# Second scores and new values that wait for fewer VectorE operations, and squares' sums in two pieces

## The reference, cut to what matters

```python
def l2norm(x):
    return x * lax.rsqrt(jnp.sum(x * x, axis=-1, keepdims=True) + EPS)

def gated_delta_rule(q, k, v, g, beta):        # q, k: l2norm of silu(conv(h @ w))
    G = jnp.cumsum(gc, axis=-1)
    decay = jnp.exp(jnp.where(incl, G[..., :, None] - G[..., None, :], -jnp.inf))
    kk = jnp.einsum("bhnid,bhnjd->bhnij", kc, kc)
    a_mat = jnp.where(strict, bc[..., :, None] * kk * decay, 0.0) + jnp.eye(CHUNK)
    sol = lax.linalg.triangular_solve(a_mat, rhs, left_side=True, lower=True, unit_diagonal=True)
    u, w = sol[..., :dv], sol[..., dv:]
    qk = jnp.einsum("bhnid,bhnjd->bhnij", qc, kc) * decay
    def step(state, xs):
        v_new = u_n - jnp.einsum("bhck,bhkv->bhcv", w_n, state)
        o_n = jnp.einsum("bhck,bhkv->bhcv", q_n, state) + jnp.einsum("bhij,bhjv->bhiv", qk_n, v_new)
        state = state * gl_n[..., None, None] + jnp.einsum("bhck,bhcv->bhkv", k_n, v_new)
        return state, o_n
```

## Time and profile before

| | us |
|---|---|
| three timed runs, median (lowest to highest) | 887.73 (886.16 to 887.88) |
| the profiled execution, its own time | 888.88 |
| its span, first to last instruction | 887.10 |
| TensorE busy (share of the span) | 862.4 (97%) |
| VectorE, ScalarE, GpSimd busy | 501.6, 470.4, 474.0 |

### The profile page before, as it was taken

One profiled execution on the slowest core, in us unless ns is written; L12 is line 12 of the kernel. 1 busy time (PEld: TensorE's weight loads), 2 busy tenths in 40 slices (PEclk: granted clock), 3 DMA queues, 4 the chain that ended last, 5 costly groups with the idle time before them and its releaser, 6 DMA issues.

```text
span 887.1 us, 16449 instructions
## 1 busy us (share of the span) xinstructions
PE 862.4 (97%) x6363; PEld 769.9 (87%) x6363; DVE 501.6 (57%) x997; ACT 470.4 (53%) x745; POOL 474.0 (53%) x372
## 2 busy tenths in 40 slices
PE   8999999999999999899999999999999999999995
PEld 7989888999999997689899998989989888888884
DVE  2923254772221327541598734434648689999983
ACT  5454254644544656754357332233545668778763
POOL 5975755989988987585754342344679000000000
PEclk9999999999999999999999998999999999999998
DMA  8643434555555454443423212133353589999931
GB/s 328 220 169 134 149 100 163 184 172 207 195 189 192 180 191 142 143 143 143 143 96 106 86 55 90 50 103 131 144 192 122 223 317 349 363 377 344 373 141 47
DMA packets 23566, 159.62 MB, mean 180 GB/s; under 512 B 3008, under 2 KB 3536, under 8 KB 4816
## 3 DMA queue, kind: packets, MB, share of 16 engines
q1 hardware_dynamic: 21456, 154.67, 48.7%
q10 hardware_dynamic: 2048, 4.07, 1.2%
HBM read 157.68 MB, written 1.05 MB: 179 GB/s over the span
## 4 chain that ended last, share of the span: by engine, by line
PE 87%; DVE 7%; ACT 2%; DMA 2%; issue 1%; ACTq 0%; SPq 0%; DVEq 0%
PE bank L1144 71%; PE bank L1695 3%; PE bank L1900 1%; DVE work L2189 1%; DMA row<-dt_bias_dram 1%; PE bank L1289 1%; PE bank L2017 1%; DMA raw<-weights_dram 1%; PE bank L1338 1%; DVE bank L2514 1%; PE bank L1300 1%; PE bank L1242 1%; PE bank L1532 1%; PE bank L1770 1%; PE bank L1705 1%
## 5 line engine op out<-in xcount | busy, mean ns | idle before, releaser
L587 POOL TENSOR_TENSOR w_lo<-raw,w_hi 128x512 fp32r<-128x512 f32 x368 | 473.8, 1326 | 215.1 <-ACT w_hi L628 214.8
L1144 PE MATMUL bank<-h_hi,w_hi 128*128 128x256 f32 x856 | 251.2, 293 | 1.9 <-DVE h_lo L2116 1.4
L1144 PE MATMUL bank<-h_lo,w_hi 128*128 128x256 f32 x856 | 244.1, 285 | 0.0
L1144 PE MATMUL bank<-h_hi,w_lo 128*128 128x256 f32 x856 | 244.1, 285 | 0.0
L628 ACT ACTIVATE w_hi<-raw 128x1024 fp32r<-128x1024 f32 x184 | 188.4, 1058 | 78.4 <-PE bank L1144 44.3
L1144 PEld LDWEIGHTS bank<-h_hi,w_hi 128*128 128x128 f32 x856 | 165.9, 194 | 7.3 <-issue 2.5
L1144 PEld LDWEIGHTS bank<-h_lo,w_hi 128*128 128x128 f32 x856 | 166.1, 194 | 0.9 <-issue 0.5
L1144 PEld LDWEIGHTS bank<-h_hi,w_lo 128*128 128x128 f32 x856 | 166.0, 194 | 0.0
L1144 PE MATMUL bank<-w_hi,g_hi 128*128 128x512 f32 x208 | 81.7, 393 | 0.0
L1144 PE MATMUL bank<-w_hi,g_lo 128*128 128x512 f32 x208 | 81.2, 390 | 0.0
L1144 PE MATMUL bank<-w_lo,g_hi 128*128 128x512 f32 x208 | 81.1, 390 | 0.0
(11 more groups left out here) (400 smaller groups left out, 1414.8 us busy)
## 6 DMA issues: line engine op xcount, KB each, us to landing
raw<-weights_dram SPq DMA_DIRECT2D x119, 1024.0 KB, 4.9
spare<-weights_dram SPq DMA_DIRECT2D x18, 1024.0 KB, 5.9
tok<-weights_dram SPq DMA_DIRECT2D x9, 1024.0 KB, 5.1
x_sb<-x_dram SPq DMA_DIRECT2D x2, 512.0 KB, 4.5
work<-final_norm_dram ACTq DMA_DIRECT2D x2, 512.0 KB, 4.9
work<-constants_dram ACTq DMA_DIRECT2D x1, 640.0 KB, 5.2
con<-constants_dram ACTq DMA_DIRECT2D x1, 584.0 KB, 3.9
out_dram<-tok SPq DMA_DIRECT2D x1, 512.0 KB, 2.7
```

The source lines that it names most:

```text
L587: ins = nc.gpsimd.tensor_tensor(w_lo[:, part], raw[:, part], w_hi[:, part].bitcast(F32), ALU.subtract)
L1144: ins = mm(dst, a, b, start=start and n == 0, stop=stop and n == 2, skip_group_check=True)
```

## The change

In the sums: `square_sums(i)` does q's half (i = 0) in the middle of tick 22 and k's half (i = 1) in the middle of tick 23, 16 matmuls each. ScalarE makes q's two squares in tick 21. `root` waits for both halves.

In the decay of t = 1: ScalarE takes the exponentials of bank 7 first. VectorE masks bank 7 in the step "decay" and bank 6 only behind "begin". TensorE's second scores wait for all but the last two operations of each group (`LATE_MASKS`), which are these. VectorE's own scores step waits for them itself.

In the old state: VectorE does the new values of both groups, then the outputs' parts of both, then the states of both. TensorE's "new c" for c of 2 and 3 waits only for the first of these operations in each group. VectorE's new state waits for the rest itself, and TensorE waits for them once more before the warming matmuls ahead of `mix_turn(0)`, which write bank 4.

```diff
+LATE_MASKS = 2
@@ ScalarE
-                    for b, name in ((6, "near"), (7, "near_t")):
+                    for b, name in ((7, "near_t"), (6, "near")) if t else ((6, "near"), (7, "near_t")):
...
-                act_e.wait_ge(sem("square_sums"), 1)
+                act_e.wait_ge(sem("square_sums"), 2)
...
-                if tick == 22:
-                    for i in range(4):
-                        act_e.wait_ge(sem("silu_done"), 4)
+                if tick in (21, 22):
+                    for i in range(2 * (tick - 21), 2 * (tick - 21) + 2):
+                        act_e.wait_ge(sem("silu_done"), i + 1)
                         nc.scalar.square(squares[i], (aq, ak)[i // 2][:, 2 * (i % 2):2 * (i % 2) + 2, :])\
                             .then_inc(sem("squared"), 1)
+                if tick == 22:
                     conv2_first(2, av, (0, 1))
@@ TensorE
+                if tick == HEAD_TICK + HEAD_PAIRS - 1:
+                    square_sums(0)
                 if tick == HEAD_TICK + HEAD_PAIRS:
-                    square_sums()
+                    square_sums(1)
...
-            def square_sums():
+            def square_sums(i):
                 pe.wait_ge(sem("negated_ready"), 4 * HEADS)
-                pe.wait_ge(sem("squared"), 4)
+                pe.wait_ge(sem("squared"), 2 * i + 2)
                 for t in range(NT):
-                    for f in range(8):
+                    for f in range(4 * i, 4 * i + 4):
...
-            def delta_await(n, groups):
+            def delta_await(n, groups, late=0):
                 for g in groups:
                     pe.wait_ge(sem(f"delta_scalar{g}"), delta_count(DELTA_SCALAR, DELTA_SLOTS[:n]))
-                    pe.wait_ge(sem(f"delta_vector{g}"), delta_count(DELTA_VECTOR, DELTA_SLOTS[:n]))
+                    pe.wait_ge(sem(f"delta_vector{g}"), delta_count(DELTA_VECTOR, DELTA_SLOTS[:n]) - late)
...
-                delta_await(n, (0, 1) if stage == "scores" else (g,))
+                delta_await(n, (0, 1) if stage == "scores" else (g,), LATE_MASKS if stage == "scores" and t else 0)
...
             def new_values(n, c):
-                delta_await(n, (0, 1))
+                if c < 2:
+                    delta_await(n, (0, 1))
+                else:
+                    for g in range(2):
+                        pe.wait_ge(sem(f"delta_scalar{g}"), delta_count(DELTA_SCALAR, DELTA_SLOTS[:n]))
+                        pe.wait_ge(sem(f"delta_vector{g}"), delta_count(DELTA_VECTOR, DELTA_SLOTS[:n - 1]) + 1)
...
                     if i == 1 and f == 0:
+                        for g in range(2):
+                            pe.wait_ge(sem(f"delta_vector{g}"), delta_count(DELTA_VECTOR, DELTA_SLOTS[:-1]))
                         keep_warm(4, 4)
@@ VectorE
-            def second_decay(n, t):
-                for b in (6, 7):
-                    for g in range(2):
-                        dve.wait_ge(sem(f"delta_scalar{g}"), delta_count(DELTA_SCALAR, DELTA_SLOTS[:n + 1]) + b - 7)
+            def second_decay(n, t, b):
+                for g in range(2):
+                    dve.wait_ge(sem(f"delta_scalar{g}"), delta_count(DELTA_SCALAR, DELTA_SLOTS[:n + 1]) + 6 - b)
...
             def delta_decay(n, t):
                 if t:
-                    return second_decay(n, t)
+                    return second_decay(n, t, 7)
...
             def delta_begin(n, t):
...
+                if t:
+                    second_decay(n - 1, t, 6)
...
                 if stage == "scores":
+                    if t:
+                        dve.wait_ge(sem(f"delta_vector{g}"), delta_count(DELTA_VECTOR, DELTA_SLOTS[:n]))
...
             def old_state(n, c):
-                for g in range(2):
-                    own, done = slice(HD * g, HD * g + HD), sem(f"delta_vector{g}")
+                groups = [(g, slice(HD * g, HD * g + HD), sem(f"delta_vector{g}"), bank[4 + 2 * g]) for g in range(2)]
+                for g, own, done, cross in groups:
                     dve.wait_ge(sem(f"delta_ready{g}"), n + 1)
-                    cross = bank[4 + 2 * g]
                     V.tensor_tensor(four(v_new[rows, g, :]), delta[t][g]["u"][rows, :, :], four(cross[rows, 0:S]),
                                     ALU.subtract).then_inc(done, 1)
+                for g, own, done, cross in groups:
                     V.tensor_tensor(four(o_tmp[rows, g, :]), four(cross[rows, S:512]), spread(exp_g[rows, t, g:8:2], HD),
                                     ALU.mult).then_inc(done, 1)
-                    if c < 3:
+                if c < 3:
+                    for g, own, done, cross in groups:
...
             def new_state(n, c):
+                if c >= 2:
+                    for g in range(2):
+                        dve.wait_ge(sem(f"delta_vector{g}"), delta_count(DELTA_VECTOR, DELTA_SLOTS[:n]))
```

More of the change, by code:

```diff
@@ L2555, in norm_qk @@
                     .then_inc(sem("qk_normed"), 1)
-            def second_decay(n, t):
-                for b in (6, 7):
-                    for g in range(2):
-                        dve.wait_ge(sem(f"delta_scalar{g}"), delta_count(DELTA_SCALAR, DELTA_SLOTS[:n + 1]) + b - 7)
-                    for g in range(2):
-                        d, done, of = delta[t][g], sem(f"delta_vector{g}"), bank_part(b, S * g, CHUNK)
-                        for name, mask in ((("far", "far_c"), ("near", "near_c")), (("qk_t", "tri_c"), ("near_t", "near_tc")))[b - 6]:
-                            V.tensor_tensor(d[name], of, each_of(con[:, CON[mask]], 4), ALU.mult).then_inc(done, 1)
+            def second_decay(n, t, b):
+                for g in range(2):
+                    dve.wait_ge(sem(f"delta_scalar{g}"), delta_count(DELTA_SCALAR, DELTA_SLOTS[:n + 1]) + 6 - b)
+                for g in range(2):
+                    d, done, of = delta[t][g], sem(f"delta_vector{g}"), bank_part(b, S * g, CHUNK)
+                    for name, mask in ((("far", "far_c"), ("near", "near_c")), (("qk_t", "tri_c"), ("near_t", "near_tc")))[b - 6]:
+                        V.tensor_tensor(d[name], of, each_of(con[:, CON[mask]], 4), ALU.mult).then_inc(done, 1)
             def delta_decay(n, t):
                 if t:
-                    return second_decay(n, t)
+                    return second_decay(n, t, 7)
                 for g in range(2):
```

## The result

The changed kernel takes 877.37 us (median of four runs, 876.87 to 877.68), the kernel before, timed beside it, 886.94 (885.20 to 887.88): ratio 0.9894, 95% interval 0.9875 to 0.9912. It is 9.6 us faster by the medians; the forecast was 878.5 within 876.0 to 884.5. The profiled execution took 877.62 us, 11.3 less than the one before; its span is 875.7. Of the 52 timed executions of the kernel before, in this comparison and the later ones, two (900.39 and 901.50 us) stand some 13 us above the rest, as do two of `p1` (893.96, 897.56) and one of `best2` (891.10), and the ratios leave these five out.

A forecast was written before the change was run, and what follows sets the result against it. TensorE was taken as the bound, with time to regain only from its waits and low-clock stretches. 2.4 + 5.25 + 3.25 - 0.2 = 10.7 us off 888.88 gave 878.2, stated as 878.5, range 876.0 to 884.5.

The forecast's parts named there:

- part 1: Sums in two pieces of 16: 2.4 us gained up to the roots' spreading, bounds 1.1 and 3.4.
- part 2: Second scores, four masks made late: squaring 5.25 us earlier, 1.33 from the wait, the rest clock; bounds 1.3 and 5.6.
- fourth powers of the second chunk: Cost of the old state's reordering in the second chunk: 0.2 us later, 0.9 if a product meets GpSimd.
- part 3: Old state reordered, third new values waiting for less: fourth old state 3.25 us earlier, bounds 1.8 and 3.4.
- all three falls: Low clock stretches at the sums, second scores and third new values: 6.9, 10.2 and 3.4 us.
- the next stall: After the second scores' half quarter, TensorE waits 0.35 us for VectorE's eight operations before the new values.
- just not late: VectorE's four new-state operations after the old state end at 596.95, just before the fourth old state at 597.05.
- A: The forecast: the clock stays up at all three places, 876.5 to 880.5 us; chance 0.55.
- B: One thin place left, at sums' first piece or roots' spreading: one clock fall, 880 to 882.5 us; chance 0.25.
- C: Clock falls don't hang on these waits and move elsewhere; only waits come back: 3.9 us, 885; chance 0.10.
- D: VectorE becomes the bound, TensorE waits in "fourth" and before every new values: under 1.8 us left, 887.5; chance 0.05.
- E: Slower: TensorE waits at the shifted roots, clock falls ahead of the first delta stages, 889.5 or 895; chance 0.05.

The follow-up runs named there:

- p1: Kernel before with only the sums in two pieces: 881.81 us median, ratio 0.9939.
- best2: Changed kernel, second chunk's old state by groups, fourth old state waiting for less, three wide matmuls in the wait at 366 us: ratio 0.9882.
- warm_waits: Kernel before with four wide matmuls in each wait, ahead of second scores and third new values, neither shortened: 882.67 us, ratio 0.9956.
- p1_warm: Kernel before with the sums in two pieces and four wide matmuls in each of the two waits, neither shortened: 879.73 us, ratio 0.9914.
- warm_sums: Kernel before with four wide matmuls in all among the sums: ratio 0.9996.
- late0: Changed kernel with LATE_MASKS = 0, so the second scores again wait for all of VectorE's operations: 883.23 us median, ratio 0.9950.
- p2: Kernel before with only the second scores' changes (order of exponentials and masks, LATE_MASKS): 883.72 us median, ratio 0.9953.
- p3: Kernel before with only the changes of old state, new values and their two waits: 884.11 us median, ratio 0.9969.

## Why the prediction was right, point by point

**Sum.** By passages of the chain of waits, in us gained:

| | forecast | measured | of it clock |
|---|---|---|---|
| part 1, sums to first transposes | 2.4 | 3.11 | up to 3.11 |
| part 2, start of the scores | 1.33 | 1.33 (43.00 to 41.67 from the transposes) | 0 |
| part 2, scores to squaring | 3.9 | 3.85 | 3.85 |
| fourth powers of the second chunk | -0.2 | -0.37 | 0 |
| part 3, third to fourth old state | 3.25 | 2.94 | 1.48 |
| sum | 10.7 | 10.9 | up to 8.4 |

The spans differ by 11.4; 0.45 of the rest arose ahead of the sums, where the change does nothing. Taking the sum from 888.88, the profiled execution's time, gave 878.2. The timed runs of the kernel before lie 1.0 to 3.7 us lower than its profiled one, in the median 1.9; those of the changed kernel at most 0.8. That difference was part of the gain, as argued: the profiled execution had all three falls, and its mean clock, 0.983, is the lowest that any of the 46 has. So the 10.7 is the gain over a bad execution, and over the typical one it is 9.6. The forecast time didn't suffer, since it was taken from the same bad execution. The 0.3 between 878.2 and 878.5 had no reason of its own.

**Part 1.** Right, with one term too large. The masks were to take 3.5 us; they took 2.7, all eight at 0.33 from 481.15 on. GpSimd's pair of subtractions had ended (477.92 to 480.44), and the next began at 483.45, with the last mask. So the first norming starts at 491.54 (491.99 in the prediction's count, which runs 0.45 us later here), not 493.1, and TensorE meets it nearly without a wait. The first piece of the sums didn't wait.

**Part 2.** Right to 0.1 us: the start by four masks of 0.33, their cover by the first group's scores, and the next stall. It is where it was said to be, in front of the first new values, with 0.5 us (0.35 forecast). But this isn't new: p1 has it as well, so in the kernel before the slow clock hid it. One argument for the clock was weaker than it looked. A slice at 9 doesn't show that a wait of 1.4 us left the clock up, since the fall of 3.4 us at 368 us lies in a slice that reads 9 too. The windows of the same trace do show it: 1.00 at that wait.

**Part 3.** The stall that was "just not late" was late by 0.4. VectorE's state products ended at 587.13, which is the forecast 595.5 in the old count (8.37 us later). The four operations behind them were to take 1.45 us and took 1.73; they end at 588.86, when TensorE has waited 0.4 for them. VectorE's timeline there:

```profile
585.19 1.94 DVE L2659 TENSOR_TENSOR work<-work,exp_g 64x256 f32<-64x256 f32 x2
587.21 0.87 DVE L2674 TENSOR_TENSOR work<-work,bank 64x256 f32<-64x256 f32 x2
588.11 0.75 DVE L2681 TENSOR_TENSOR tok<-bank,work 64x256 f32<-64x256 f32 x2
```

The loss at the fourth powers was 0.37, not 0.2: the two more operations ahead of group 0's state product cost 0.67, and that product, 0.73 us before, now took 0.43, which gives back 0.30 and not the 0.46 that the forecast's 0.2 implies.

**Rivals.** A happened. B: no thin place was left; nine executions of the changed kernel lie within 876.87 and 878.78. C: the gain without any wait shortened (warm_waits, p1_warm) refutes it. The Trainium skill (TensorE: Matmul & The Clock Gate, HAM oscillation) ties falls to longer waits than 2 us; the falls behind waits of 2.0 and 1.8 us here decide against it. D: the new waits of TensorE are 0.5, 0.4 and 0.4 us, a small part of what it needed. E: nothing of it seen.

**Where the reasoning was too simple.** The prediction spoke of the clock's falls as if each wait caused its own. The profiles of p1 and warm_sums kept it up through waits of 2.0 and 1.8 us, that of late0 through one of 2.0. What the change removes is the chance of a fall, and the profiled execution of before was one in which all three fell. The Trainium skill (the same page, Part 1: The HAM clock gate) calls the chip's watch on activity free-running: it doesn't start anew with the kernel. The runs agree as far as they go: the same code has the fall in one execution and not in the next (p1 with a mean clock of 0.996 and of 0.986), and a part that moves a place in time (p1) changes what happens at places behind it. What decides in the single case was not tested. It stays open, too, why the falls stay away in half of p1's executions and in none of the kernel before's.

## What to carry to other kernels

A wait of TensorE of about 2 us in front of thin matmuls can cost more than itself: here 3.85 us of clock for 1.33 of waiting taken away. Price both, and look at the granted clock of the passage before counting the wait. Where a wait can't be shortened, a few wide matmuls into a free bank gave back most of it. Since falls come and go between executions, compare passages of several profiles, not spans of two, read the mean granted clock of every timed execution, and don't expect parts to add up.

In an order of operations for one consumer, put first what it reads, but check each user of the same order: the reordering that helped the third new values delayed the second chunk's fourth powers.

## What the hardware showed that was not expected

- The clock falls without any wait, at 32 matmuls of two columns (0.77 over 15 us in the earlier trace rows; the profiles of p2, p3 and warm_waits have the fall too). It is at 1.00 in every profile in which they come as 16 and 16 with projections of 256 columns between.
- A VectorE operation with two operands in SBUF took 1.35 us beside GpSimd and 0.41 without; shifted by 1.3 us, all eight are of the short kind. Not each one beside GpSimd is slow: the last of the eight started just behind one of GpSimd's in the changed kernel and kept its 0.41. A shift can be worth as much as an operation saved.
